# One-hots of the dense tokens' gates: from VectorE and ScalarE to GpSimd

## The chip, the cores and the metric

The kernel runs on one core of a Trainium2 chip. The metric is the device time of one execution in microseconds, lower is better. The time of the kernel before is 4674.65 us, the median of 3 runs (4665.11 to 4679.74).

## What is computed

One inference step of a decoder trunk with one layer: a convolution branch and a gated linear attention branch are merged and added to the input, and then comes a mixer with very many small experts (PEER). 512 prompt tokens and 64 sample tokens, 2048 channels, all float32. The change lies in the mixer:

```python
v1, i1 = lax.top_k(s1, 16)          # s1, s2: scores against 128 keys each, per token and head
v2, i2 = lax.top_k(s2, 16)
cs, ci = lax.top_k(v1 + v2 over all pairs, 16)
e = i1[ci // 16] * 128 + i2[ci % 16]          # 16 experts of 16384 for each of 8 heads
g = jax.nn.softmax(cs)
act = gelu(einsum('tkd,td->tk', u_tab[e], h))
out = einsum('tk,tkd->td', g * act, v_tab[e])
```

So each token uses 128 experts, each with a gate g. A matrix "gate of expert e for token t" has 16384 x tokens entries, 128 of them non-zero per token; expert e is the pair (i1, i2) of two numbers under 128.

## The kernel before

The mixer treats the tokens in two ways, both at the same time.

**Gathered tokens** (256 of the prompt, and 64 more packed as a third tile): for each of a token's 128 experts the row of 2048 numbers is fetched by an indirect DMA, one for 128 tokens at once, into a ring of slots. There are 641 such rows. GpSimd issues the gathers (`gather`, L2044) in order; before each it waits until the row that last lay in the slot has been used. The ring has four slots for the first 264 rows and three after that. VectorE uses the rows: L966 multiplies and sums a u row, L974 adds a weighted v row.

**Dense tokens** (256): all 16384 experts are computed, in 128 blocks of 128 experts. In block b TensorE multiplies the block's part of peer_u with the normed tokens (L738, 16 products of 128x128 by 128x256, each of which shows as two in the records), and GELU follows on ScalarE and VectorE: ScalarE squares (L1911), VectorE L1498, ScalarE Tanh (L1918), VectorE L1512 or L1515, and the result H of the block stays in SBUF. After block 127 the v phase follows (L758), with H as operand. The uT loads come in halves of 512 KB on SyncE's queue (L2253) into the four slots of RA, and so do the peer_v loads (L2255).

**Gates of the dense tokens**: from block G_AT = 63 on, TensorE makes the gate matrix of four tokens behind the u product of each block (L749): for one token the product of two one-hot matrices over its 128 selected experts. One has a 1 at i2 of each, the other the gate at i1; their product has the gate of expert (i1, i2) at its place. The one-hots lie in `ohs`, two buffers (halves) of two tokens, each with two kinds (0: scaled by the gate, 1: plain). They take the fourth slot of RA, so that in this stage uT halves have three. `selT` holds the indices and gates with the selected experts on the partitions, and `iota128` the numbers 0 to 127 in each. Per block and half VectorE compares once for both tokens and kinds (`onehots`, L1478, 128x512), and ScalarE scales kind 0 with the gate by two Copy activations (L1927), and then signals `oh_scaled`. The one-hots of gate step q = b + 1 - G_AT are made in block b, for TensorE in block b + 1; they wait until the gate product of block b has read the buffers before. ScalarE copies the gates out of PSUM (L1915) for the blocks ahead, and VectorE multiplies them into H for the blocks behind (`gate_tokens`, L1488) and, for the block at hand, L1522.

**What sets the order.** The order of each engine is fixed in the program. TensorE: u product of b, gate product, u product of b + 1. Both take the next of four PSUM banks (`banks.take`), which must have been freed: a u product's by `h_ready`, a gate product's by `gm_ready`, both of VectorE. VectorE in block b of this stage: `gate_tokens`, L1498, the one-hots, L1512/L1515, L1522, and then as many rows of the gathered tokens as a credit allows (`paced(work, 4.2)`, a row costs 2.4), one or two. How many rows fall into which block is thus settled when the program is built. GpSimd in this stage has the gathers alone, with a query load, a residual load and a gain load where a tile of gathered tokens ends.

Of the kernel before, what the change touches and what calls it, by code (L numbers as in the profile page):

```python
# [9 lines left out]
ACT = mybir.ActivationFunctionType  # L10
ALU = mybir.AluOpType
AX = mybir.AxisListType

P = 128
# [25 lines left out]
NB = NEXP // P  # L40
# [5 lines left out]
G_AT = NB - ND // 4 - 1  # L46
# [87 lines left out]
def trunk(nc, a, o, seen, final):  # L134
    ctx = ExitStack()
    with ctx:
        def sb(name, shape, dt=F32):
            return ctx.enter_context(nc.sbuf_tensor(name, shape, dt))
# [11 lines left out]
        iota128 = sb("iota128", [P, P])  # L150
# [22 lines left out]
        at = KC  # L173
# [83 lines left out]
        selT = holes[:, 0:12, :].rearrange("p (k h) c -> p k h c", k=3)  # L257
# [7 lines left out]
        ohs = [part_of(RA, 3072 + 512 * i, 2, 2, P) for i in range(2)]  # L265
# [24 lines left out]
        def signal(name):  # L290
# [4 lines left out]
        ps_done, z_ready, scores_ready, kdT_ready, o_ready, os_ready, u_half, v_half, w_half = (  # L295
            signal(s) for s in ("ps_done", "z_ready", "scores_ready", "kdT_ready", "o_ready", "os_ready", "u_half",
                                "v_half", "w_half"))
# [14 lines left out]
        (dve_step, ms1_ready, normT_ready, lg_ready, earg_ready, factors_ready, kdarg_ready, decay_ready, att_ready,  # L312
         rsilu_ready, state_ready, kdm_ready, st_updated, gla_ready, head_zeroed, u_ready, conv_done, centered,
         sd_ready, lned, silu_ready, mergedB_ready, part_ready, merged_ready, resid_ready, ms2_ready, h2_ready,
         routed, shifted, gates_ready, row_used, gelu_arg, ss_g, y_g, arg_u, h_ready, onehot_ready, gm_ready,
         sum_ready, ms3_ready, y_ready, sums_ready) = (
            signal(s) for s in (
                "dve_step", "ms1_ready", "normT_ready", "lg_ready", "earg_ready", "factors_ready", "kdarg_ready",
                "decay_ready", "att_ready", "rsilu_ready", "state_ready", "kdm_ready", "st_updated", "gla_ready",
                "head_zeroed", "u_ready", "conv_done", "centered", "sd_ready", "lned", "silu_ready", "mergedB_ready",  # L320
                "part_ready", "merged_ready", "resid_ready", "ms2_ready", "h2_ready", "routed", "shifted",
                "gates_ready", "row_used", "gelu_arg", "ss_g", "y_g", "arg_u", "h_ready", "onehot_ready", "gm_ready",
                "sum_ready", "ms3_ready", "y_ready", "sums_ready"))

        pool_step, consts_made, iota_made, masks_made, qk_zeroed, qs_zeroed = (
# [18 lines left out]

        banks = Banks(ps, signals, seen, final)
        gelu_due = {}
        weight_order = []
        weight_spent = []

# [12 lines left out]
        own_last = max(m for m in range(2 * G_AT - 2) if slot_of[m] == 3)  # L362
# [428 lines left out]
        def _(dve):  # L791
# [673 lines left out]
                    spare((g, hd, "wq"), (16.0, 12.0)[g])  # L1465


            def onehots(q):
                if q == 0:
                    for t in range(2):  # L1470
                        dve.wait_ge(*selT_ready.at(t))
                    dve.wait_ge(*ps_done.at("u", own_last // 2))
                else:
                    dve.wait_ge(*ps_done.at("g", q - 1))
                for half in range(2):
                    t, n = q // 32, q % 32 * 4 + 2 * half
                    sel = selT[:, 0:2, 2 * t + n // 64, n % 64:n % 64 + 2]
                    onehot_ready.on(dve.tensor_tensor(  # L1478
                        ohs[half], iota128[:, :].unsqueeze(1).unsqueeze(1).to_broadcast([P, 2, 2, P]),
                        sel.unsqueeze(3).to_broadcast([P, 2, 2, P]), ALU.is_equal), q, half)  # L1480


            def gate_tokens(q, n):
                dve.wait_ge(*ps_done.at("g", q))
                dve.wait_ge(*g_copied.at(q))
# [6 lines left out]
            for b in range(NB):  # L1492
                scratch = H[:, b, :] if b <= G_AT else u_work
                bank = banks.of("u", b)
                if b > G_AT:
                    gate_tokens(b - 1 - G_AT, b)
                dve.wait_ge(*sq_u.at(b))
                arg_u.on(dve.scalar_tensor_tensor(out=scratch, in0=scratch, scalar=1.0, in1=bank[:, 0:ND], op0=ALU.add,  # L1498
                                                  op1=ALU.mult), b)
                spare((b, "u"), 0.0)  # L1500
                if b < G_AT - 1:
                    paced(work_1, 3.9)
                    paced(work, 2.8)
                elif b < NB - 2:
                    onehots(b + 1 - G_AT)
                assert b != G_AT - 4 or next(work_1, None) is None
                assert b != G_AT or first_row[1] < row_used.n
                assert b != H_FOURTH - 1 or row_used.n >= FOUR_ROWS
                dve.wait_ge(*tanh_u.at(b))
                done = 4 * max(b - G_AT, 0)  # L1510
                if done:
                    dve_step.on(dve.scalar_tensor_tensor(out=scratch[:, 0:done], in0=scratch[:, 0:done], scalar=1.0,  # L1512
                                                         in1=bank[:, 0:done], op0=ALU.add, op1=ALU.mult))
                if done < ND:
                    ins = dve.scalar_tensor_tensor(out=H[:, b, done:], in0=scratch[:, done:], scalar=1.0,  # L1515
                                                   in1=bank[:, done:ND], op0=ALU.add, op1=ALU.mult)
                if 0 < done < ND:
                    dve_step.on(ins)
                if done:
                    dve.wait_ge(*g_copied.at(b - 1 - G_AT))  # L1520
                    dve.wait_ge(*dve_step.now())
                    ins = dve.tensor_tensor(H[:, b, 0:done], scratch[:, 0:done], H[:, b, 0:done], ALU.mult)  # L1522
                h_ready.on(ins, b)
                banks.free(h_ready, "u", b)
                if G_AT - 1 <= b < NB - 3:
                    paced(work, 4.2)
# [24 lines left out]
        def _(act):  # L1551
            fn = nc.scalar.activation
# [350 lines left out]
            for b in range(NB):  # L1903
                serve((b, "u"))
                scratch = H[:, b, :] if b <= G_AT else u_work
                act.wait_ge(*ps_done.at("u", b))
                if b > G_AT:
                    act.wait_ge(*h_ready.at(b - 1))
                if b == H_FOURTH:
                    act.wait_ge(*row_used.at(FOUR_ROWS - 1))  # L1910
                sq_u.on(fn(scratch, banks.of("u", b)[:, 0:ND], ACT.Square, scale=float(np.sqrt(0.044715))), b)  # L1911
                if b > G_AT:
                    q = b - 1 - G_AT
                    act.wait_ge(*ps_done.at("g", q))
                    g_copied.on(fn(H[:, b:, 4 * q:4 * q + 4],  # L1915
                                   banks.of("g", q).rearrange("p (n i) -> p i n", n=4)[:, b:, :], ACT.Copy), q)
                act.wait_ge(*arg_u.at(b))
                tanh_u.on(fn(scratch, scratch, ACT.Tanh, scale=float(np.sqrt(2.0 / np.pi))), b)  # L1918
                if b == G_AT - 1:
                    sel_keep()  # L1920
                if G_AT - 1 <= b < NB - 2:
                    q = b + 1 - G_AT
                    for half in range(2):
                        act.wait_ge(*onehot_ready.at(q, half))
                        for n in range(2):
                            c = q % 32 * 4 + 2 * half + n
                            ins = fn(ohs[half][:, 0, n, :], ohs[half][:, 0, n, :], ACT.Copy,  # L1927
                                     scale=selT[:, 2, 2 * (q // 32) + c // 64, c % 64:c % 64 + 1])
                        oh_scaled.on(ins, q, half)


            ones_made.on(fn(iota128[:, :], iota128[:, :], ACT.Copy, scale=0.0, bias=1.0))
# [14 lines left out]
        def _(pool):  # L1947
# [45 lines left out]
            def query_load(t):  # L1993
                if t:
                    pool.wait_ge(*y_g.at(before_tile[t]))
                else:
                    pool.wait_ge(*normT_ready.at(1, KT - 1))
                    pool.wait_ge(*x2_stored.at(0))
                n = TOK[t]
                src = (h2_d[0], h2_d[1], h2_d[2, 0:OWN, :])[t]  # L2000
                if t >= 2:
                    pool.wait_ge(*x2_stored.at(1))
                    pool.wait_ge(*h2_stored.at(1))
                for i in range(P // n):
                    key = (t, i) if i < P // n - 1 else (t,)
                    query_in.dma(pool.dma_start(h2cur[i * n:(i + 1) * n, :], src), *key)
                if t:
                    last = before_tile[t]
                    yg_stored.dma(pool.dma_start(y_out[last], cur[0:TOK[last], :]), last)
# [15 lines left out]
            def gather(m):  # L2025
# [13 lines left out]
                if kind == "m":  # L2039
# [5 lines left out]
                    ring[s][:, :], None, (a["peer_u"] if kind == "u" else a["peer_v"])[0],  # L2045
                    bass.IndirectOffsetOnAxis(ap=idx, axis=0), bounds_check=NEXP - 1, oob_is_err=True), m)

            query_load(0)
            for m in range(len(row_list)):
                t = row_list[m][0]  # L2050
                gather(m)
                if m - 3 == last_u[t]:
                    gain_load(t)
                if t and m == first_row[t] + 2:
                    query_load(t)
                if m == first_row[t] + 12:
                    residual_load(t)
# [287 lines left out]
```

## Time and profile before

| | before |
|---|---|
| median of 3 runs | 4674.65 us |
| lowest and highest run | 4665.11, 4679.74 us |
| span of the profiled execution | 4667.9 us |
| TensorE busy | 4588.6 us (98%) |
| VectorE busy | 2713.5 us (58%) |
| ScalarE busy | 539.6 us (12%) |
| GpSimd busy | 956.5 us (20%) |
| DMA moved | 1350.34 MB, 289 GB/s in the mean |

The profile is of one execution, and its own time stands in the table as the span. Busy shares are means over stages that differ much; the stage of the change is the part from 3217 to 3740 us. There are stages before it in which GpSimd and the gathers do nothing, and behind it the v phase, with DMA at its fullest.

### The profile page before, as it was taken

To read this page: it belongs to the slowest core of one execution; us is meant where nothing else is said; L and a number is where in the kernel's file an instruction comes from. 1 tells how busy PE (TensorE), PEld (TensorE's weight loads), DVE (VectorE), ACT (ScalarE), POOL (GpSimd) and SP (SyncE) were. 2 spreads that over 40 slices of the span, in tenths; PEclk is the share of its full clock that TensorE was granted. 3 is DMA by queue.
4 is the path that set the end of the run, shared out by engine and by line. 5 is a ranking of instruction groups with operands and counts; after the bars stand their busy time and mean duration, and the time that the engine had idled before them with its cause. 6 is when DMAs were issued, how large, how long until landed. Compare 5 with 4: busy or idle time off the path is not lost.

```text
span 4667.9 us, 50792 instructions
## 1 busy us (share of the span) xinstructions
PE 4588.6 (98%) x20474; PEld 3719.0 (80%) x20474; DVE 2713.5 (58%) x4679; ACT 539.6 (12%) x1229; POOL 956.5 (20%) x691
## 2 busy tenths in 40 slices
PE   8999999999999999999999999999999999999998
PEld 7888888888767676667776678888888888888887
DVE  4434500017678686745556658886788855556552
ACT  1111200000111111010000111112222200000000
POOL 1000000000112313014443332222332323222220
PEclk9999999999999999999999999999999999999999
DMA  4434444545669779659999888888999999999994
GB/s 174 139 133 140 172 147 155 176 172 178 219 237 334 290 266 350 221 211 361 362 370 377 332 327 327 329 332 323 346 356 345 348 380 410 395 413 420 421 417 164
DMA packets 264157, 1350.34 MB, mean 289 GB/s; under 512 B 45729, under 2 KB 52129, under 8 KB 140338
## 3 DMA queue, kind: packets, MB, share of 16 engines
q1 hardware_dynamic: 170066, 663.90, 38.9%
q0 software_dynamic: 93856, 683.19, 37.0%
q8 instruction: 162, 2.65, 0.2%
q14 instruction: 73, 0.60, 0.0%
HBM read 1306.30 MB, written 40.16 MB: 288 GB/s over the span
## 4 chain that ended last, share of the span: by engine, by line
PE 87%; DMA 8%; DVE 3%; issue 1%; ACT 0%; POOL 0%; DVEq 0%; POOLq 0%; ACTq 0%
PE ps L404 39%; PE ps L738 16%; PE ps L758 9%; PE pm L758 9%; PE ps L563 4%; DMA RA<-in_uT 4%; PE ps L625 2%; DMA RA<-in_peer_v 2%; DMA RING<-in_peer_u,table 2%; PE ps L518 1%; PE pm L511 1%; PE pm L467 1%; PE ps L571 1%; DVE BIG L1252 1%; DMA BIG<-in_peer_v,table 1%
## 5 line engine op out<-in xcount | busy, mean ns | idle before, releaser
L404 PE MATMUL ps<-X,BIG 128*128 128x320 f32 (+1 forms) x5632 | 1394.9, 409 | 7.5 <-DVE X L1444 4.2
L404 PEld LDWEIGHTS ps<-X,BIG 128*128 128x128 f32 x5632 | 1068.4, 190 | 317.6 <-issue 10.0
L738 PE MATMUL ps<-X,RA 128*128 128x256 f32 x4096 | 902.2, 380 | 20.9 <-DMA RA<-in_uT 20.7
L738 PEld LDWEIGHTS ps<-X,RA 128*128 128x128 f32 x4096 | 772.6, 190 | 131.6 <-DMA RA<-in_uT 22.6
L974 DVE SCALAR_TENSOR_TENSOR CUR<-RING,wexp,CUR 128x2048 f32<-128x2048 f32 x288 | 676.8, 2350 | 258.0 <-DMA RING<-in_peer_v,table 150.3
L966 DVE CUSTOM_DVE_ANT_0 RING<-RING,CUR 128x2048 f32<-128x2048 f32 x286 | 652.0, 2289 | 280.0 <-DMA RING<-in_peer_u,table 146.9
L2044 POOL DMA_INDIRECT RING<-in_peer_u,table x222 | 352.3, 1587 | 951.1 <-DVE hidden L966 644.0
L2044 POOL DMA_INDIRECT RING<-in_peer_v,table x224 | 332.1, 1483 | 920.1 <-DVE CUR L974 746.5
L404 PE MATMUL ps<-BIG 128*128 128x256 f32 (+1 forms) x2048 | 504.4, 408 | 7.9 <-DVE BIG L1430 5.6
L404 PEld LDWEIGHTS ps<-BIG 128*128 128x128 f32 x2048 | 389.9, 191 | 117.8 <-DVE BIG L1430 7.0
L758 PE MATMUL ps<-BIG,RA 128*128 128x256 f32 x2048 | 465.4, 380 | 8.7 <-DMA RA<-in_peer_v 8.7
L758 PE MATMUL pm<-BIG,RA 128*128 128x256 f32 x2048 | 463.4, 379 | 1.5 <-DVE BIG L1488 1.3
L758 PEld LDWEIGHTS ps<-BIG,RA 128*128 128x128 f32 x2048 | 389.6, 191 | 64.9 <-DMA RA<-in_peer_v 11.9
L758 PEld LDWEIGHTS pm<-BIG,RA 128*128 128x128 f32 x2048 | 388.6, 190 | 56.2 <-DMA RA<-in_peer_v 1.8
L1345 DVE SCALAR_TENSOR_TENSOR BIG<-BIG,ps 128x256 f32<-128x256 f32 (+1 forms) x32 | 14.6, 455 | 426.0 <-PE ps L404 426.0
L1252 DVE SCALAR_TENSOR_TENSOR BIG<-BIG 128x256 f32<-128x256 f32 x720 | 240.4, 412 | 0.1
L563 PE MATMUL ps<-BIG,X 128*128 128x256 f32 x1024 | 223.4, 379 | 0.0
L563 PEld LDWEIGHTS ps<-BIG,X 128*128 128x128 f32 x1024 | 194.2, 190 | 28.2 <-issue 1.5
L1984 POOL MEMSET BIG<- 128x1024 f32 x1 | 1.0, 952 | 914.5 <-DVE BIG L1362 914.5
L404 PE MATMUL ps<-RA,BIG 128*128 128x256 f32 (+1 forms) x512 | 128.6, 410 | 3.9 <-issue 3.9
L404 PEld LDWEIGHTS ps<-RA,BIG 128*128 128x128 f32 x512 | 98.1, 192 | 32.1 <-issue 5.9
L625 PE MATMUL ps<-BIG 128*128 128x256 f32 x512 | 110.8, 379 | 1.3 <-DVE BIG L1362 1.3
(317 smaller groups left out, 3082.5 us busy)
## 6 DMA issues: line engine op xcount, KB each, us to landing
BIG<-in_w_in_b SPq DMA_DIRECT2D x128, 1024.0 KB, 5.8
RA<-in_uT SPq DMA_DIRECT2D x256, 512.0 KB
RA<-in_peer_v SPq DMA_DIRECT2D x256, 512.0 KB
BIG<-in_w_gb_b SPq DMA_DIRECT2D x32, 1024.0 KB, 5.1
BIG<-in_w_ga_b SPq DMA_DIRECT2D x32, 1024.0 KB, 4.9
BIG<-in_w_gla_o_b SPq DMA_DIRECT2D x32, 1024.0 KB, 5.0
BIG<-in_w_mix_b SPq DMA_DIRECT2D x32, 1024.0 KB, 6.7
BIG<-in_w_q_b SPq DMA_DIRECT2D x32, 1024.0 KB, 8.1
```

What stands on the lines that cost most here:

```text
L404: last = pe.matmul(bank[:, 0:n], w(k, j * P, P), src[:, k, 0:n], start=(k == 0), stop=(k == kt - 1))
L467: last = pe.matmul(lev_ps[0:n, l, 0:n], kk, qq, start=(j == 0), stop=(j == 1))
L511: last = pe.matmul(pm[0:NS, 2, :], qs[:, j, b * NS:(b + 1) * NS], sring[:, b % 4, j, :], start=False, stop=(b == DEC_B - 1 and j == 1))
L518: last = pe.matmul(bank, kdm[0:NS, b % 2, j * P:(j + 1) * P], vt[0:NS, 2, :], start=True, stop=True)
L563: last = pe.matmul(bank[:, c * PAIR:(c + 1) * PAIR], normT[g][:, k, span(c)], w(k, 0, PAIR), start=(k == 0), stop=(k == KT - 1))
L625: last = pe.matmul(bank[:, c * PAIR:(c + 1) * PAIR], merged[0][:, k, span(c)], w(k, 0, PAIR), start=(k == 0), stop=(k == KT - 1))
L738: last = pe.matmul(bank[:, 0:ND], half_slot[slot_of[m]][:, k % 8, :], h2T[1][:, k, 0:ND], start=(k == 0), stop=(k == KT - 1))
L758: last = pe.matmul(v_sums[half][:, i, :], vhalf[slot_of[m]][:, i * P:(i + 1) * P], H[:, b, :], start=(b == 0 and i % 2 == 0), stop=(b == N ...
L966: row_used.on(dve.tensor_tensor_reduce(out=row, in0=row, in1=h2cur[0:n, :], scale=1.0, scalar=0.0, op0=ALU.mult, op1=ALU.add, accum_out=hi ...
L974: row_used.on(dve.scalar_tensor_tensor(out=cur[0:n, :], in0=row, scalar=wexp[0:n, par, k:k + 1], in1=cur[0:n, :], op0=ALU.mult, op1=ALU.ad ...
L1252: ins = dve.scalar_tensor_tensor(out=out, in0=src, scalar=w, in1=out, op0=ALU.mult, op1=ALU.add)
L2044: row_loaded[s].dma(pool.indirect_dma_start(ring[s][:, :], None, (a["peer_u"] if kind == "u" else a["peer_v"])[0], bass.IndirectOffsetOnAx ...
```

## The change

The comparisons leave VectorE and the scalings leave ScalarE. GpSimd makes each 128x128 one-hot by one tensor_scalar: iota128 is compared with the index on each partition, and for kind 0 a second operation of the same instruction multiplies with the gate. That is 8 instructions per block instead of 2 on VectorE and 4 on ScalarE. They wait for the same things as before (the gate product that read the buffers last) and signal `oh_scaled` themselves. When VectorE's program is built, it notes at each place where the one-hots were how many rows it has used (`rows_before_onehot`). GpSimd's program puts the one-hots in front of the first gather whose number is over that: with m rows used, the gather of row m still goes ahead of them, and the gather of row m + 1 comes behind.

```diff
-            def onehots(q):
-                ...
-                    dve.wait_ge(*ps_done.at("g", q - 1))
-                for half in range(2):
-                    t, n = q // 32, q % 32 * 4 + 2 * half
-                    sel = selT[:, 0:2, 2 * t + n // 64, n % 64:n % 64 + 2]
-                    onehot_ready.on(dve.tensor_tensor(
-                        ohs[half], iota128[:, :].unsqueeze(1).unsqueeze(1).to_broadcast([P, 2, 2, P]),
-                        sel.unsqueeze(3).to_broadcast([P, 2, 2, P]), ALU.is_equal), q, half)
...
                 elif b < NB - 2:
-                    onehots(b + 1 - G_AT)
+                    rows_before_onehot.append(row_used.n)
...
-                if G_AT - 1 <= b < NB - 2:
-                    q = b + 1 - G_AT
-                    for half in range(2):
-                        act.wait_ge(*onehot_ready.at(q, half))
-                        for n in range(2):
-                            c = q % 32 * 4 + 2 * half + n
-                            ins = fn(ohs[half][:, 0, n, :], ohs[half][:, 0, n, :], ACT.Copy,
-                                     scale=selT[:, 2, 2 * (q // 32) + c // 64, c % 64:c % 64 + 1])
-                        oh_scaled.on(ins, q, half)
...
+            def onehots(q):
+                if q == 0:
+                    for t in range(2):
+                        pool.wait_ge(*selT_ready.at(t))
+                    pool.wait_ge(*ps_done.at("u", own_last // 2))
+                else:
+                    pool.wait_ge(*ps_done.at("g", q - 1))
+                for half in range(2):
+                    for n in range(2):
+                        c = q % 32 * 4 + 2 * half + n
+                        at = 2 * (q // 32) + c // 64, c % 64
+                        for kind in range(2):
+                            gate = selT[:, 2, at[0], at[1]:at[1] + 1] if kind == 0 else None
+                            ins = pool.tensor_scalar(
+                                ohs[half][:, kind, n, :], iota128[:, :], selT[:, kind, at[0], at[1]:at[1] + 1], gate,
+                                ALU.is_equal, *((ALU.mult,) if kind == 0 else ()))
+                    oh_scaled.on(ins, q, half)
...
             for m in range(len(row_list)):
                 t = row_list[m][0]
+                while q < len(rows_before_onehot) and m > rows_before_onehot[q]:
+                    onehots(q)
+                    q += 1
                 gather(m)
```

## Rows read from the trace of the kernel before

**Rows 1.** The page: busy time (share of the span) and instructions of each engine.

```profile
PE 4588.6 (98%) x20474; PEld 3719.0 (80%) x20474; DVE 2713.5 (58%) x4679; ACT 539.6 (12%) x1229; POOL 956.5 (20%) x691
```

**Rows 2.** The page: the chain of work that ended last, by engine.

```profile
PE 87%; DMA 8%; DVE 3%; issue 1%; ACT 0%; POOL 0%; DVEq 0%; POOLq 0%; ACTq 0%
```

**Rows 3.** Gate products: ns min/median/max, first and last start; in 3217:3737 busy, mean | idle.

```profile
L749 PE MATMUL ps<-RA x512: 272/275/275, 3220.9 to 3740.3; 128*128 128x128 f32 x171
...
L749 PE MATMUL ps<-RA 128*128 128x128 f32 x504 | 66.4, 275 | 0.0
```

**Rows 4.** The chain in order of time, 3395 to 3440: start us, us, what.

```profile
3399.21 3.72 PE ps L738 x16
3402.93 0.89 PE ps L749 x8
3403.82 6.91 PE ps L738 x32
...
3430.71 8.38 DMA RA<-in_uT
```

**Rows 5.** Waits in 3217:3737: engine line <- releaser: us in total, times, longest us.

```profile
DVE RING L966 <- DMA RING<-in_peer_u,table: 23.0, 14, 2.9
...
PE ps L738 <- DMA RA<-in_uT: 19.1, 19, 2.2
...
DVE CUR L974 <- DMA RING<-in_peer_v,table: 9.3, 6, 3.0
```

**Rows 6.** Timeline of one block: start us, us, engine, line, what [idle before <- releaser].

```profile
3406.35 2.28 DVE L966 CUSTOM_DVE_ANT_0 RING<-RING,CUR 128x2048 f32<-128x2048 f32 x1
...
3408.57 2.29 DVE L966 CUSTOM_DVE_ANT_0 RING<-RING,CUR 128x2048 f32<-128x2048 f32 x1
3409.44 2.29 POOL L2044 DMA_INDIRECT RING<-in_peer_u,table  x1 [5.21 <-DVE hidden L966]
...
3411.44 0.52 DVE L1488 TENSOR_TENSOR BIG<-ps,BIG 128x344 f32<-128x344 f32 x1 [0.58 <-issue]
...
3411.87 0.41 DVE L1498 SCALAR_TENSOR_TENSOR table<-table,ps 128x256 f32<-128x256 f32 x1
3412.04 1.01 POOL L2044 DMA_INDIRECT RING<-in_peer_u,table  x1 [0.30 <-issue]
3412.20 1.29 DVE L1478 TENSOR_TENSOR RA<-iota,X 128x512 f32<-128x512 f32 x2
3412.32 0.42 ACT L1918 ACTIVATE table<-table 128x256 f32<-128x256 f32 x1 [0.97 <-DVE table L1498]
...
3413.40 0.24 DVE L1512 SCALAR_TENSOR_TENSOR table<-table,ps 128x92 f32<-128x92 f32 x1
...
3414.16 2.29 DVE L966 CUSTOM_DVE_ANT_0 RING<-RING,CUR 128x2048 f32<-128x2048 f32 x1
...
3417.60 2.29 DVE L966 CUSTOM_DVE_ANT_0 RING<-RING,CUR 128x2048 f32<-128x2048 f32 x1 [1.15 <-DMA RING<-in_peer_u,table]
```

**Rows 7.** The stage: us, busy us (instructions) of each engine, TensorE clock, DMA share, GB/s.

```profile
3217.00:3737.00 520.00, 500.75 (x2528) 440.81 (x2528) 422.89 (x623) 144.76 (x447) 158.13 (x109) 1.00 0.92 347
```

**Rows 8.** Groups in 3217:3737: shapes, count | busy us, mean ns | idle before, releaser.

```profile
L966 DVE CUSTOM_DVE_ANT_0 RING<-RING,CUR 128x2048 f32<-128x2048 f32 x58 | 132.0, 2288 | 23.1 <-DMA RING<-in_peer_u,table 23.0
L974 DVE SCALAR_TENSOR_TENSOR CUR<-RING,wexp,CUR 128x2048 f32<-128x2048 f32 x51 | 119.8, 2349 | 11.0 <-DMA RING<-in_peer_v,table 9.3
...
L1927 ACT ACTIVATE RA<-RA,X 128x128 f32<-128x128 f32 x256 | 82.9, 394 | 13.0 <-DVE RA L1478 13.0
L1478 DVE TENSOR_TENSOR RA<-iota,X 128x512 f32<-128x512 f32 x128 | 82.7, 687 | 1.4 <-ACT X L1873 1.3
```

**Rows 9.** GpSimd's arithmetic of the size: ns min/median/max, first and last start.

```profile
L1977 POOL COPY BIG<-ident x1: 292/292/292, 14.3 to 14.3; 128x128 f32<-128x128 f32 x1
...
L1975 POOL TENSOR_SCALAR_AFFINE_SELECT BIG<-BIG x12: 294/370/714, 8.3 to 13.5; 128x128 f32<-128x128 f32 x12
```

**Rows 10.** Timeline of VectorE near the end: the last row of the gathered tokens.

```profile
4560.71 2.35 DVE L974 SCALAR_TENSOR_TENSOR CUR<-RING,wexp,CUR 128x2048 f32<-128x2048 f32 x1 [1.35 <-DMA RING<-in_peer_v,X]
```

More of the change, by code:

```diff
@@ L314, in trunk @@
          sd_ready, lned, silu_ready, mergedB_ready, part_ready, merged_ready, resid_ready, ms2_ready, h2_ready,
-         routed, shifted, gates_ready, row_used, gelu_arg, ss_g, y_g, arg_u, h_ready, onehot_ready, gm_ready,
+         routed, shifted, gates_ready, row_used, gelu_arg, ss_g, y_g, arg_u, h_ready, gm_ready,
          sum_ready, ms3_ready, y_ready, sums_ready) = (
@@ L321, in trunk @@
                 "part_ready", "merged_ready", "resid_ready", "ms2_ready", "h2_ready", "routed", "shifted",
-                "gates_ready", "row_used", "gelu_arg", "ss_g", "y_g", "arg_u", "h_ready", "onehot_ready", "gm_ready",
+                "gates_ready", "row_used", "gelu_arg", "ss_g", "y_g", "arg_u", "h_ready", "gm_ready",
                 "sum_ready", "ms3_ready", "y_ready", "sums_ready"))
@@ L346, in trunk @@
         gelu_due = {}
+        rows_before_onehot = []
         weight_order = []
@@ L1465, in _ @@
                     spare((g, hd, "wq"), (16.0, 12.0)[g])
-            def onehots(q):
[L1469 to L1473, printed above, removed]
-                    dve.wait_ge(*ps_done.at("g", q - 1))
-                for half in range(2):
-                    t, n = q // 32, q % 32 * 4 + 2 * half
-                    sel = selT[:, 0:2, 2 * t + n // 64, n % 64:n % 64 + 2]
-                    onehot_ready.on(dve.tensor_tensor(
-                        ohs[half], iota128[:, :].unsqueeze(1).unsqueeze(1).to_broadcast([P, 2, 2, P]),
-                        sel.unsqueeze(3).to_broadcast([P, 2, 2, P]), ALU.is_equal), q, half)
             def gate_tokens(q, n):
@@ L2046, in gather @@
                     bass.IndirectOffsetOnAxis(ap=idx, axis=0), bounds_check=NEXP - 1, oob_is_err=True), m)
+            def onehots(q):
[15 more added lines that the diff above has]
+                    oh_scaled.on(ins, q, half)
             query_load(0)
+            q = 0
             for m in range(len(row_list)):
                 t = row_list[m][0]
+                while q < len(rows_before_onehot) and m > rows_before_onehot[q]:
+                    onehots(q)
+                    q += 1
                 gather(m)
```

## Prediction

> **What bounds the kernel now.** I read the page first. TensorE is busy in 98% of the span [rows 1] and holds 87% of the chain that ended last [rows 2], so only what delays TensorE costs time. The change touches one stage, the 64 expert blocks 63 to 126, in which each block has an up-projection product (L738) and then a gate product (L749) that reads the one-hots. The first of its 512 gate matmuls starts at 3220.9 us and the last at 3740.3 [rows 3], so 63 periods take 519.4 - 0.9 = 518.5 us, 8.23 us each. The chain shows an undisturbed period: 0.89 us of L749 and 6.91 of L738, 7.80 us [rows 4]. The other 0.43 us per block, 27 us in all, are TensorE's waits for the uT loads, 19.1 us of idle [rows 5], and the restarts behind them (the half product behind a load takes 3.72 us, against half of 6.91 [rows 4]). TensorE never waited for a one-hot or for a bank: neither stands among the waits of the stage, and L749 has no idle time in front of it [rows 3, 5]. So **the comparisons and the scaling are hidden today**, and removing them cannot by itself give anything.
>
> Then I looked at what the three engines do in a block [rows 6]. VectorE is busy 423 of 520 us [rows 7], and its largest work is one or two expert rows per block (L966, L974; 58 and 51 rows in the stage, 1.7 per block, 2.3 us each [rows 8]). GpSimd does only gathers, 109 of them [rows 7], and spends most of its time waiting for a ring slot. Each row needs its gather, and there are three slots.
>
> **What is removed.** VectorE loses 128 comparisons of 0.687 us, two per block, which take 1.29 us together; ScalarE loses 256 scalings of 0.394 us [rows 6, 8]. Where they overlap they are busy for 82.7 and 82.9 us of the stage [rows 8]. In the block of [rows 6] the first comparison starts when L1498 ends; without the two, L1512 would wait for the Tanh only, which ends at 3412.74, and start at 3412.8, not 3413.4. The u product ended at 3410.73 [rows 4], so VectorE's first row starts 2.9 us after it and not 3.4. All this lies beside TensorE: gain 0.
>
> **What is added.** GpSimd gets 8 tensor_scalar of 128x128 per block. The trace has none. Nearest rows on GpSimd: the copy of 128x128 takes 0.292 us, and an affine select of that size 0.294 to 0.714 in 12 cases, 0.370 in the median [rows 9]. A comparison against a per-partition value is nearest to the select, and half of the new instructions do a second operation; I take **0.40 us**, a little over the median select, and keep 0.29 and 0.71 as ends. Eight are 3.2 us (2.3 to 5.7).
>
> They don't run undisturbed. A gather takes 1.00 us when VectorE does no row, but 2.29 us when it comes up in the middle of one: that of 3409.44 ends at 3411.73, 0.9 us after the row that ran to 3410.86; the next, at 3412.04, takes 1.01 [rows 6]. So a GpSimd instruction that reads SBUF is held until a row operation, with its two inputs in SBUF, is through. I take the same for the new ones, since they read iota128 and selT: a row in their midst adds up to 2.3 us. The Trainium skill has this as a rule (SBUF — State Buffer, Who interferes with whom: a VectorE instruction with two SBUF inputs contends with a GpSimd instruction that reads SBUF); for the gathers this trace agrees, for arithmetic no row shows it. By the rule 8 one-hots need 3.2 to 5.5 us, without it 3.2.
>
> **The new wait, and what is queued behind it.** GpSimd now waits in each block for the gate product, because the one-hot buffers are single. On its in-order queue the gathers stand behind. With m the first row that VectorE uses in block b, the order is gather m, one-hots, gather m+1 (and m+2). Today gather m+1 goes out 0.8 us after its slot is free; a gather that was released at 3408.65 is used at 3417.60, and that row still waited for its data, 1.15 us [rows 6]. In the change gather m+1 goes out only after one-hots, some 5 to 7 us later, and VectorE's second row of the block, then its whole next block (banks of u and g), wait for it. Who waits for that: a u product takes the bank of the u product two blocks back, freed by VectorE. The query, residual and gain loads on that queue keep their places against rows already used, and cost nothing. SyncE's queue isn't touched.
>
> I walk seven blocks with 2, 2, 1, 2, 2, 1 rows, as the stage has them. Terms: u 6.91, g 0.89; VectorE's work before its rows ends 2.9 after the u product, or takes 2.25 when VectorE is late (0.52 + 0.41, 0.6 for the Tanh, 0.76 from L1512 to the row, less gaps); row 2.3; gather 1.0, 0.3 to the next, landing 5.9 after its end (3411.73 to 3417.60); 0.8 from a freed slot to the gather [rows 6]. Zero is the end of a u product. Block 0: g to 0.89, one-hots from 1.15, held by the row of 3.15 to 5.45, done at 6.65; gather of the second row ends 7.65 and lands 13.55; that row ends 15.85 (today about 8). Block 1: VectorE frees its bank at 18.0, while TensorE wants it at 16.5; the g product of block 2 has to wait until 16.35, for a bank, the next u product until 18.0. One-hots of block 2 lie between rows and end at 25.55, 0.65 after TensorE wants them. Carried on, the u products end at 0, 7.8, 15.6, 24.9, 33.4, 41.2, 49.3: in the mean **8.22**, that is 0.42 of new wait per block over 7.80. Most of it is for banks, some for one-hots, and behind a single-row block VectorE catches up.
>
> Of today's 0.43 us for the uT loads some goes under these waits, since a standing TensorE lets loads land. DMA is 92% busy in the stage [rows 7], so not all of it goes: I let two thirds stay, 0.29. Sum: 7.80 + 0.42 + 0.29 = 8.51, against 8.23: 0.28 x 63 = **+17.6 us**. Behind the stage nothing changes: the plan hands the same rows to the same blocks, and the last row ends at 4563, 105 us before the span does [rows 10]. The profiled execution of before spans 4667.9 us, 6.75 under the median 4674.65 of its runs; I add that: 4674.65 + 17.6 = 4692.
>
> **The rivals.**
> Heavy: GpSimd becomes the bound. It decides from about 0.5 us per instruction. Then its own work per block is 8 x 0.5 = 4.0, 1.7 gathers x 1.45 (158 us over 109 [rows 7]) = 2.5, and 2.3 held by a row: 8.8 us, +0.57 x 63 = +36 us; at 0.71 it is 5.7 + 2.5 + 2.3 = 10.5, +143 us. I set it at +60: 4735. For it: half of the new instructions have two operations, and both take two pointers' worth of operands. Against it: 0.292 for the copy. 22%.
> Hidden: 0.3 us per instruction or no hold by rows. Then one-hots are ready 2.4 to 3.2 us after g, gather m+1 lands by 11.5, the row ends 13.8, the bank is free at 16.0, before 16.5. New waits vanish, and the time is 4675, within 5. 26%.
> Faster: the same small price, and the gathers, held back by one-hots, leave uT loads a freer path. Its place is the three-slot ring of uT halves, whose loads stand on the chain for 8.38 us [rows 4] where two halves and at most one g product give 6.9 to 7.8. It decides if a load gets 0.6 us shorter; it gives at most the 27 us, and I price it at two thirds, -18: 4657. Against it: the bytes per block stay, and two gathers in a bunch load DMA more at once. 14%.
> My forecast of +17.6 has 38%, its own range +5 to +35.
>
> **How the numbers follow.** 0.3%, about what a measurement of this kernel can tell from no change, is 14 us. Slower: the heavy case and four fifths of the forecast's, 0.22 + 0.30 = 0.52. Same: the hidden case and the rest, 0.34. Faster: 0.14. For 8 in 10 the range goes down to 4660, into the faster case, and up to 4750, which leaves out the upper third of the heavy one.
>
> **What would show it.** L749 with idle in front of it, released by GpSimd, means late one-hots; L738 with idle from a VectorE release means banks, so late gathers. DMA idle in front of L966 and L974, 32 us in the stage [rows 5], should grow to over 150. The new POOL group should show 512 instructions at 0.40 us, longer ones beside rows. The first to last start of L749 should be 536 us. If the mean is under 0.3, or TensorE's clock (1.00 in the mean now, the higher of its two levels [rows 7]) falls in the new waits, I am wrong in size; if the DMA waits of L738 vanish without new ones, in sign.

## The result, and the profile after

The changed kernel takes 4830.18 us (median of 4 runs, 4823.18 to 4832.06), the kernel before in the same comparison 4677.01 us (median of 4). The ratio is 1.0335, with a 95% interval of 1.0322 to 1.0349: **153 us slower**, where 17.6 were forecast and the range ended at 4750.

The page of the kernel after: the busy row, and the chain that ended last by engine and by line (rows 1 and 2 of before). Lines have moved: L739 is L738 of before, L750 is L749, L967 and L975 are L966 and L974, L2021 is L2044, and L2038 is the new tensor_scalar.

```profile
PE 4654.4 (96%) x20474; PEld 3756.8 (78%) x20474; DVE 2646.4 (55%) x4551; ACT 456.3 (9%) x973; POOL 1442.0 (30%) x1203
...
PE 78%; POOL 11%; DMA 5%; DVE 3%; issue 3%; ACT 0%; DVEq 0%; POOLq 0%; ACTq 0%
PE ps L405 37%; PE ps L739 9%; POOL RA L2038 9%; PE ps L759 9%; PE pm L759 8%; PE ps L564 4%; PE ps L626 2%; DMA RING<-in_peer_u,table 2%; POOL RING L2021 2%; DMA RA<-in_peer_v 2%; PE ps L519 1%; PE pm L512 1%; PE pm L468 1%; PE ps L572 1%; DVE BIG L1253 1%
```

GpSimd wasn't on the chain before [rows 2] and now holds 11% of it, and TensorE's share of the chain went from 87 to 78%.

The gate products of after (ns min/median/max, first and last start), and the groups of the stage, 3217 to 3900 us (count | busy us, mean ns of one | idle before them and its releasers):

```profile
L750 PE MATMUL ps<-RA x512: 272/275/582, 3221.9 to 3898.8; 128*128 128x128 f32 x171
...
L2038 POOL TENSOR_SCALAR RA<-iota,X 128x128 f32<-128x128 f32 x512 | 507.7, 1001 | 16.3 <-ACT X L1859 11.8 <-PE ps L750 1.6
...
L967 DVE CUSTOM_DVE_ANT_0 RING<-RING,CUR 128x2048 f32<-128x2048 f32 x58 | 135.0, 2327 | 148.7 <-DMA RING<-in_peer_u,table 148.5 <-issue 0.2
L975 DVE SCALAR_TENSOR_TENSOR CUR<-RING,wexp,CUR 128x2048 f32<-128x2048 f32 x51 | 122.2, 2395 | 134.0 <-DMA RING<-in_peer_v,table 133.9
L750 PE MATMUL ps<-RA 128*128 128x128 f32 x512 | 91.6, 313 | 111.1 <-POOL RA L2038 56.5 <-DVE BIG L1474 54.1
```

The stage accounts for nearly all of the loss. First to last start is 676.9 us, less 0.9 and over 63: a **period of 10.73 us**, where before it was 8.23 [rows 3]; 2.5 x 63 = 157.5 us of the 162.4 by which the profiled span is longer. The last gate matmul begins 158.5 us later than in before. The tensor_scalars take 1.00 us in the mean, and L750, which never waited [rows 3], now has 111 us of idle in front of it, half released by GpSimd (late one-hots) and half by VectorE (a gate bank not free).

The stage as a whole (length, busy us and instructions of PE, PEld, DVE, ACT and POOL, clock, DMA share, GB/s), its first half:

```profile
3217.00:3560.00 343.00, 286.23 (x1287) 242.75 (x1287) 173.34 (x249) 32.50 (x97) 326.75 (x315) 0.93 0.75 266
```

GpSimd is busy 95% of it; in before it was 158 us of 520 [rows 7]. VectorE fell from 81 to 51%, DMA from 92 to 75%. So **GpSimd is the bound of the stage**. TensorE's granted clock went from 1.00 to 0.93 of its higher level; a u product behind a wait took 8.80 us where others take 7.07. That can have cost next to nothing: from 3217 to 3900 us GpSimd's one-hots waited for a gate product 1.6 us in all, and its gathers for VectorE 2.1.

GpSimd in two blocks of after, the rows of VectorE that lie in them and a u product (timeline: start us, us, engine):

```profile
3439.61 5.48 POOL L2038 TENSOR_SCALAR RA<-iota,X 128x128 f32<-128x128 f32 x8
3444.83 2.29 DVE L967 CUSTOM_DVE_ANT_0 RING<-RING,CUR 128x2048 f32<-128x2048 f32 x1 [6.17 <-DMA RING<-in_peer_u,table]
...
3448.37 1.03 POOL L2021 DMA_INDIRECT RING<-in_peer_u,table  x1 [0.30 <-issue]
...
3449.13 2.37 DVE L967 CUSTOM_DVE_ANT_0 RING<-RING,CUR 128x2048 f32<-128x2048 f32 x1
...
3449.27 8.80 PE L739 MATMUL ps<-X,RA 128*128 128x256 f32 x32 [0.51 <-DVE BIG L1508]
...
3449.44 11.00 POOL L2038 TENSOR_SCALAR RA<-iota,X 128x128 f32<-128x128 f32 x8
...
3452.36 2.31 DVE L967 CUSTOM_DVE_ANT_0 RING<-RING,CUR 128x2048 f32<-128x2048 f32 x1 [0.84 <-DMA RING<-in_peer_u,table]
...
3456.70 2.50 DVE L967 CUSTOM_DVE_ANT_0 RING<-RING,CUR 128x2048 f32<-128x2048 f32 x1
```

The eight of 3439.61 meet no row but for their last 0.26 us, and take 5.48 us. The eight of 3449.44 meet three rows and take 11.00. That made two things to test: what an instruction costs, and what a row beside it adds.

### The profile page after: what moved, and what is told of

It reads as the page before. It is cut to its first block, busy times and chain, and to the rows that moved or that the text cites. A ratio compares the mean times of both kernels' runs of the same rounds, so it can differ in the third digit from the quotient of the medians.

```text
span 4830.3 us, 50920 instructions
## 1 busy us (share of the span) xinstructions
PE 4654.4 (96%) x20474; PEld 3756.8 (78%) x20474; DVE 2646.4 (55%) x4551; ACT 456.3 (9%) x973; POOL 1442.0 (30%) x1203
## 4 chain that ended last, share of the span: by engine, by line
PE 78%; POOL 11%; DMA 5%; DVE 3%; issue 3%; ACT 0%; DVEq 0%; POOLq 0%; ACTq 0%
PE ps L405 37%; PE ps L739 9%; POOL RA L2038 9%; PE ps L759 9%; PE pm L759 8%; PE ps L564 4%; PE ps L626 2%; DMA RING<-in_peer_u,table 2%; POOL RING L2021 2%; DMA RA<-in_peer_v 2%; PE ps L519 1%; PE pm L512 1%; PE pm L468 1%; PE ps L572 1%; DVE BIG L1253 1%
## 5 line engine op out<-in xcount | busy, mean ns | idle before, releaser
L739 PE MATMUL ps<-X,RA 128*128 128x256 f32 x4096 | 935.5, 391 | 3.5 <-DVE BIG L1508 3.4
L739 PEld LDWEIGHTS ps<-X,RA 128*128 128x128 f32 x4096 | 800.9, 197 | 120.3 <-DVE BIG L1508 5.8
L975 DVE SCALAR_TENSOR_TENSOR CUR<-RING,wexp,CUR 128x2048 f32<-128x2048 f32 x288 | 679.1, 2358 | 383.3 <-DMA RING<-in_peer_v,table 272.2
L967 DVE CUSTOM_DVE_ANT_0 RING<-RING,CUR 128x2048 f32<-128x2048 f32 x286 | 654.8, 2297 | 399.3 <-DMA RING<-in_peer_u,table 262.6
L2021 POOL DMA_INDIRECT RING<-in_peer_u,table x222 | 343.5, 1547 | 748.8 <-DVE hidden L967 481.8
L2021 POOL DMA_INDIRECT RING<-in_peer_v,table x224 | 318.0, 1420 | 771.9 <-DVE CUR L975 614.3
L2038 POOL TENSOR_SCALAR RA<-iota,X 128x128 f32<-128x128 f32 x512 | 507.7, 1001 | 16.3 <-ACT X L1859 11.8
L750 PE MATMUL ps<-RA 128*128 128x128 f32 x512 | 91.6, 313 | 111.1 <-POOL RA L2038 56.5
L750 PEld LDWEIGHTS ps<-RA 128*128 128x128 f32 x512 | 75.7, 209 | 132.9 <-POOL RA L2038 65.4
```

The lines of the kernel that those rows point to most:

```text
L739: last = pe.matmul(bank[:, 0:ND], half_slot[slot_of[m]][:, k % 8, :], h2T[1][:, k, 0:ND], start=(k == 0), stop=(k == KT - 1))
L750: last = pe.matmul(bank[:, n * P:(n + 1) * P], ohs[n // 2][:, 1, n % 2, :], ohs[n // 2][:, 0, n % 2, :], start=True, stop=True)
L967: row_used.on(dve.tensor_tensor_reduce(out=row, in0=row, in1=h2cur[0:n, :], scale=1.0, scalar=0.0, op0=ALU.mult, op1=ALU.add, accum_out=hi ...
L975: row_used.on(dve.scalar_tensor_tensor(out=cur[0:n, :], in0=row, scalar=wexp[0:n, par, k:k + 1], in1=cur[0:n, :], op0=ALU.mult, op1=ALU.ad ...
L2021: row_loaded[s].dma(pool.indirect_dma_start(ring[s][:, :], None, (a["peer_u"] if kind == "u" else a["peer_v"])[0], bass.IndirectOffsetOnAx ...
L2038: ins = pool.tensor_scalar(ohs[half][:, kind, n, :], iota128[:, :], selT[:, kind, at[0], at[1]:at[1] + 1], gate, ALU.is_equal, *((ALU.mult ...
```

## Theories

**H**, GpSimd's time: eight tensor_scalars have 5.5 us of their own, rows with two SBUF inputs hold them for 2.5 more, gathers take 2.3 and gaps 0.4, together 10.7. **L**, the order: gathers stand behind the one-hots and come too late; VectorE waits for its rows and TensorE for its banks, and the price of an instruction matters only through this. In both, the waits of after would look much the same.

## The experiments

Ratios are against the kernel before on the same chip, with 95% intervals. The period is worked out as above, from the first and last start of the gate products.

**One-input rows.** On the changed kernel; the two one-hots also stand on lines of their own here and below, L2032 with two operations and L2034 with one.

```diff
-row_used.on(dve.tensor_tensor_reduce(out=row, in0=row, in1=h2cur[0:n, :], ...
+row_used.on(dve.tensor_reduce(hidden[0:n, par, k:k + 1], row, AX.X, ALU.add), m)
-row_used.on(dve.scalar_tensor_tensor(out=cur[0:n, :], in0=row, scalar=wexp..., in1=cur[0:n, :], ...
+row_used.on(dve.tensor_reduce(wexp[0:n, par, k:k + 1], row, AX.X, ALU.add), m)
```

> Built on the changed kernel. Every row operation of the gathered tokens (L966/L974 of before, two inputs in SBUF) is replaced by a sum over the row, one input in SBUF, of about the same length (2.1 to 2.3 us); so the hidden values and the sums of the gathered tokens are left out, their gathers and waits stay. Theory H (GpSimd is the bound of the stage, and a third of its time it is held by row operations with two SBUF inputs): the tensor_scalars fall from 1.00 us in the mean to 0.69, the price that eight in a row show when no row is near (5.48 us); GpSimd then has 5.5 + 1.7 gathers of 1.0 + 0.6 of gaps = 7.8 us per block, so the period falls from 10.7 to 8.0 to 8.4 us and the time to between 4665 and 4700 us. Theory L (the late gathers set the period, the hold is a side effect of any busy VectorE): the tensor_scalars stay near 1.0 us, the period over 9.8, the time over 4770.

Measured: 4689.93 us, ratio 1.0051 (1.0032 to 1.0069); period 8.59 us. The two lines of the tensor_scalars (ns min/median/max):

```profile
L2032 POOL TENSOR_SCALAR RA<-iota,X x256: 786/796/1025, 3214.0 to 3756.7; 128x128 f32<-128x128 f32 x128
...
L2034 POOL TENSOR_SCALAR RA<-iota,X x256: 589/591/651, 3214.8 to 3757.4; 128x128 f32<-128x128 f32 x128
```

H holds for the size of the hold: with the second SBUF input of the rows gone, 142 of the 162 us of span are gone, though VectorE still does a row operation in the same places. The period is over the 8.0 to 8.4 that I expected: VectorE still waits 143 us of 500 for rows, and the experiment with these rows and the gathers first, below, shows that this is the order. The run also gives the undisturbed price: **0.80 us with two operations, 0.59 with one**, 4 x 1.39 = 5.5 us per block. Of 8 x 1.00 us in after, 2.5 are thus hold.

**Gathers first.**

```diff
-while q < len(rows_before_onehot) and m > rows_before_onehot[q]:
+while q < len(rows_before_onehot) and m > rows_before_onehot[q] + 2:
```

> The changed kernel, but with up to two more gathers ahead of the one-hots of a block on GpSimd's queue, so that VectorE's rows of this block and the first of the next don't wait for one-hots. Theory H (GpSimd's own time is the bound, 8 one-hots x 1.0 + 1.7 gathers x 1.3): the sum is the same, so the period stays at 10.2 to 10.9 us and the time at 4800 to 4845; VectorE's waits for rows shrink and TensorE's waits for one-hots grow instead. Theory L (late gathers): the period falls under 9.3 and the time under 4745.

Measured: 4841.44 us, ratio 1.0366 (1.0337 to 1.0394); period 10.95 us, a little over the range, from two runs. As H says: the order alone gives nothing back while GpSimd's time is the bound. Its first waits of 3230 to 3730 us (engine line <- releaser: us in total, times, longest), and a stretch of the timeline of GpSimd and of VectorE:

```profile
PEld ps L750 <- POOL RA L2038: 101.5, 40, 5.5
PE ps L750 <- POOL RA L2038: 100.0, 50, 5.3
DVE RING L967 <- DMA RING<-in_peer_u,table: 67.2, 16, 6.4
```

```profile
3462.02 4.66 POOL L2036 TENSOR_SCALAR RA<-iota,X 128x128 f32<-128x128 f32 x1
3466.67 0.59 POOL L2038 TENSOR_SCALAR RA<-iota,X 128x128 f32<-128x128 f32 x1
...
3461.59 2.28 DVE L967 CUSTOM_DVE_ANT_0 RING<-RING,CUR 128x2048 f32<-128x2048 f32 x1
...
3463.80 2.28 DVE L967 CUSTOM_DVE_ANT_0 RING<-RING,CUR 128x2048 f32<-128x2048 f32 x1
```

VectorE's waits for rows fall (67 + 30 us in this window, 215 in after) and TensorE's waits for one-hots grow, 40 to 100 us. GpSimd is busy 475 of the 500 us, as in after (477). The timeline shows the hold in its clearest form: one tensor_scalar of 0.8 us takes 4.66, since two rows follow each other without a gap; it ends 0.6 us after the second. GpSimd doesn't get in between.

**Kind split.** GpSimd makes the scaled one-hots alone; VectorE compares the plain ones.

```diff
+onehot_ready.on(dve.tensor_tensor(ohs[half][:, 1, :, :], iota128 ... , sel ... , ALU.is_equal), q, half)
...
-for kind in range(2):
-    ...
-    ins = pool.tensor_scalar(ohs[half][:, kind, n, :], iota128[:, :], selT[:, kind, ...], gate, ALU.is_equal, ...)
+ins = pool.tensor_scalar(ohs[half][:, 0, n, :], iota128[:, :], selT[:, 0, ...], selT[:, 2, ...], ALU.is_equal, ALU.mult)
```

> The whole computation. GpSimd makes only the scaled one-hots (kind 0, four instructions with two operations per block, gate multiplied in), VectorE compares the plain ones (kind 1, one instruction for two tokens, 128x256), ScalarE does nothing for them. Theory H: GpSimd has 4 x 0.77 = 3.1 us of its own, up to 2.5 of hold and 1.7 x 1.3 of gathers, 7.8 us, just under TensorE's period with its load waits (8.23): 4670 to 4700 us. Theory L: the gathers still stand behind the one-hots, which end at most 2 us earlier, so that a third at least of the 153 us stays: over 4725.

Measured: 4762.19 us, ratio 1.0203 (1.0182 to 1.0224); period 9.53 us. H's 4670 to 4700 is missed, and L's "over 4725" met. GpSimd is busy 396 of 500 us and no longer the bound, and yet 95 us are lost. The four instructions take 1.23 us each: half as many, but 0.44 us of hold in each instead of 0.31, so the hold doesn't go with their number. The waits of 3230 to 3730 us:

```profile
DVE CUR L976 <- DMA RING<-in_peer_v,table: 89.0, 23, 8.4
DVE RING L968 <- DMA RING<-in_peer_u,table: 82.4, 24, 8.0
PEld ps L751 <- DVE BIG L1489: 60.0, 21, 5.6
PE ps L751 <- DVE RA L1480: 52.7, 23, 5.2
```

VectorE waits 171 us for rows, and TensorE for VectorE: for a gate bank (L1489), and for the plain one-hots (L1480) that VectorE makes again, as in before. This is L, which H had hidden.

**Kind split, gathers first.** Both edits.

> The split of the kinds again (GpSimd the scaled one-hots, VectorE the plain ones), with up to two more gathers ahead of GpSimd's one-hots. With the split alone the period was 9.53 us and GpSimd 79% busy, VectorE waiting 171 us of 500 for rows. Theory H alone (GpSimd's own time) doesn't explain that; theory L (gathers behind the one-hots come too late for VectorE, whose banks TensorE waits for) says that with the gathers ahead VectorE's waits for rows fall under 60 us, and the period to 8.2 to 8.6 us: 4665 to 4695 us. If instead the hold of GpSimd by VectorE's rows makes one-hots late, the period stays over 9.2 and TensorE's waits for GpSimd grow: over 4730.

Measured: 4725.88 us, ratio 1.0121 (1.0090 to 1.0152); period 9.09 us. Between the two expectations: VectorE's waits for rows fell to 55 us, as L said, and 36 us came back. What is left I put down to hold. From 3230 to 3730 us:

```profile
L2052 POOL TENSOR_SCALAR RA<-iota,X 128x128 f32<-128x128 f32 x221 | 340.2, 1545 | 10.2 <-PE ps L751 8.1
```

The mean tensor_scalar is now 1.55 us, GpSimd busy 451 of 500 us, and TensorE waits for it (33 us). With data at hand VectorE does its rows right behind each other; the longest tensor_scalar takes 5.19 us, so one was held for up to 4.4.

**One-input rows, gathers first.** Hold and order both taken away.

> One-input rows and the gathers ahead of the one-hots, both at once (gathered tokens' sums left out). With one-input rows alone the period was 8.59 us and VectorE waited 143 us of 500 for rows. If the two causes are GpSimd's held time and the late gathers, and no third, nothing is left: period 8.1 to 8.3 us, waits for rows under 60 us, 4660 to 4680 us. If TensorE waits for one-hots instead, since 5.5 us and two gathers come before they are ready, the period stays at 8.5 and more: over 4685.

Measured: 4676.15 us, ratio 1.0017 (1.0007 to 1.0028); period 8.25 us, against 8.23 of before [rows 3]; all as expected.

```profile
L750 PE MATMUL ps<-RA x512: 272/275/377, 3217.5 to 3738.2; 128*128 128x128 f32 x171
```

VectorE's waits for rows are 45 us of 500. So with eight tensor_scalars of 5.5 us on GpSimd the stage is as short as before once the hold and the order are gone: the two causes together are enough, and 5.5 us of own time are not by themselves too much.

**Write only.** Does a row hold every instruction of GpSimd, or those that read SBUF?

```diff
-ins = pool.tensor_scalar(ohs[half][:, kind, n, :], iota128[:, :], selT..., gate, ALU.is_equal, ...)
+for i in range(3):
+    step(pool.memset(ohs[half], 0.0))
+ins = pool.memset(ohs[half], 0.0)
```

> The changed kernel with each half's four tensor_scalars (read and write SBUF) replaced by four memsets of 128x512, each waiting for the one before (write only; so the gates and all dense experts are left out). Alone a memset of this size takes 0.52 us (0.95 for 1024 columns and 0.21 for 128, in the profile), eight of them with their waits 4.9 us per block, against 5.5 of the tensor_scalars. If VectorE's rows hold only what reads SBUF through the shared interface, the memsets stay within 10% of 0.52 us, GpSimd needs 4.9 + 2.2 of gathers, and the period is 8.3 to 8.8 us, 4675 to 4715 us, as with one-input rows. If they hold every GpSimd instruction, the memsets take 0.8 us and more in the mean and the period is over 9.5, over 4750 us.

Measured: 4718.09 us, ratio 1.0096 (1.0058 to 1.0134); period 9.04 us. The memsets (ns min/median/max), and three of them in the midst of a row:

```profile
L2034 POOL MEMSET RA<- x384: 525/525/550, 3223.0 to 3794.1; 128x512 f32 x192
L2035 POOL MEMSET RA<- x128: 525/525/528, 3224.8 to 3794.7; 128x512 f32 x128
```

```profile
3442.04 2.28 DVE L967 CUSTOM_DVE_ANT_0 RING<-RING,CUR 128x2048 f32<-128x2048 f32 x1
3442.23 1.71 POOL L2034 MEMSET RA<- 128x512 f32 x3
```

None of 512 is held, the longest takes 0.55 us. The hold is one of reads: the copies below do no arithmetic but read SBUF, and they are held. The Trainium skill says so (SBUF — State Buffer, Who interferes with whom: a VectorE instruction with two SBUF inputs contends with a GpSimd instruction that reads SBUF, not with one that only writes it). These runs agree at both ends: 1.00 us against 0.70 in the mean for tensor_scalars with two-input and one-input rows, 0.525 throughout for memsets. The time and the period are over what I expected (4675 to 4715 us, 8.3 to 8.8); I put that down to L, 158 us of waits for rows in 500. Why the period is 9.04 here and 8.59 with one-input rows stays open; the gathers, which are held here (1.31 us against 1.05), are part of it.

**Copies.** The price alone brought to the low end of my bounds.

```diff
-ins = pool.tensor_scalar(ohs[half][:, kind, n, :], iota128[:, :], selT..., gate, ALU.is_equal, ...)
+ins = pool.tensor_copy(ohs[half][:, kind, n, :], iota128[:, :])
```

> The changed kernel with each tensor_scalar replaced by a copy of 128x128 from iota128 into the same place (reads and writes SBUF as before; the comparison and the gates are left out). Alone such a copy takes 0.29 us, so this is the change at the low end of the price that I had bounded, with the two-input rows and the order of the gathers as in the change. GpSimd's own time falls from 5.5 to 2.3 us per block; with up to 2.3 of hold and 2.2 to 2.5 of gathers it isn't the bound. If the price was what decided, the period falls from 10.73 to between 8.3 and 9.1 us, what remains being the late gathers: 4675 to 4725 us. If the hold grows to fill the time (more than one row per block holds GpSimd), the period stays over 9.5 and the time over 4750.

Measured: 4685.99 us, ratio 1.0036 (1.0024 to 1.0048), 16.7 us over before; period 8.29 us.

```profile
L2037 POOL COPY RA<-iota x512: 279/288/2451, 3221.0 to 3746.3; 128x128 f32<-128x128 f32 x171
```

The hold is still there, 0.47 us in the mean where 0.29 is the price, and so is the order, but GpSimd has time for both (it is busy 347 of the 500 us from 3230): the period is within 0.1 us of before. So the price decides, through GpSimd's sum. Of the 16.7 us the stage's profile explains 8 at most. The profiled execution was the fastest of the eight, 11 us under their median, and where the others lost the rest isn't known.

**Immediates.** What of the price comes from the operands; with one-input rows. The form with one operation gets the constant 5.0 too.

```diff
-tensor_scalar(..., iota128[:, :], selT[:, 0, ...], selT[:, 2, ...], ALU.is_equal, ALU.mult)
+tensor_scalar(..., iota128[:, :], 5.0, 0.25, ALU.is_equal, ALU.mult)
```

> The kernel with one-input rows again, with the operands of the tensor_scalars as constants instead of per-partition values from selT (so the gates are left out as well). It measures what a per-partition operand costs. With them it was 0.796 us for two operations and 0.590 for one. If each costs about 0.1 us to read, the two become 0.6 and 0.5; if the loop over 128 columns is what costs (copy of 128x128: 0.29 us), they stay within 0.05 us of 0.796 and 0.590.

Measured: 0.647 us with two operations and 0.532 with one, in 4706.75 us (one run); period 8.76. So of 0.796 us two per-partition operands are 0.15, and one of 0.59 is 0.06, between my two cases. The rest is 0.29 for a copy, 0.24 more for a comparison, 0.12 for a second operation. With 15% less of its own time on GpSimd the period isn't shorter than 8.59, as fits a GpSimd that isn't the bound with one-input rows; why it is longer stays open.

**Three tries to be faster than before**, on the kernel before, by the 27 us that TensorE loses to the uT loads. The first gives fewer rows to the stage (`paced`) and more to the v phase (`V_PACE`):

```diff
-paced(work, 4.2)
+paced(work, 3.6)
-V_PACE = 3.65
+V_PACE = 3.8
```

> The kernel before with the credit of rows per block in the stage cut from 4.2 to 3.6 us and V_PACE raised from 3.65 to 3.8: some 15 rows move from the stage to the v phase. It asks what the 27 us are that TensorE loses there to uT loads. If they come from the gathers' share of the DMA (92% busy), a seventh less gathering takes away a third or more of them, and the v phase, whose rows end 105 us before the span, hides the moved rows: 4655 to 4668 us. If they come from the three-slot ring alone, 4675.

Measured: 4658.90 us, ratio 0.9977 (0.9967 to 0.9986); period 8.04 us. Of 3230 to 3730 us, TensorE's waits for loads, in before 16.9 us, are now

```profile
PE ps L738 <- DMA RA<-in_uT: 8.1, 10, 1.9
```

Faster by 9 to 11 us: a small gain clear of noise. In the stage the DMA share fell from 0.92 to 0.86. The v phase up to 4560 us was full already (0.98 to 1.01) and stays so; the rows that left the stage found room behind that, where the share rose from 0.43 to 0.69.

The second goes on, to 3.0 in the stage and from 2.8 to 3.1 before it.

> The kernel before with the rows spread further: 3.1 us of credit per block before the stage instead of 2.8, 3.0 in it instead of 4.2, V_PACE 3.8. Cutting 4.2 to 3.6 took the period of the stage from 8.23 to 8.04 us and TensorE's waits for uT loads from 19 to 8 us. If it goes on in proportion the waits fall under 3 us and the period to 7.9: 4645 to 4657 us. If the v phase is hurt by the moved rows (its DMA is 100% busy), nothing is gained over 4659.

Measured: 4685.83 us, ratio 1.0033 (1.0019 to 1.0047). The period fell on, to 7.93 us, but the time rose: 7 rows more than with 3.6 lie behind the stage, and from 4400 us on the chain that ended last is now that of the gathered rows:

```profile
by line: DMA RING<-in_peer_v,X 44.0%; DMA RING<-in_peer_u,X 18.6%; DVE CUR L974 13.6%; issue 7.4%; DVE RING L966 4.9%; PE pm L772 3.2%; DVE X L1546 2.2%; DMA RING<-CUR 1.5%; PE ps L758 1.2%; DVE CUR L970 0.8%; DVE RING L989 0.8%; DVE BIG L1
```

The third has 3.1 before the stage, 3.6 in it and `V_PACE` as it was.

> The kernel before with 3.1 us of credit before the stage and 3.6 in it, V_PACE left at 3.65. 3.6 in the stage gave 0.23% with V_PACE 3.8; 3.0 lost it again, with TensorE's waits in the last part of the v phase, where rows had been moved to. If the v phase is what limits, taking the rows into the blocks before the stage (DMA 86% busy) keeps the gain or adds to it: 4650 to 4660. If the first u blocks are no better a place, 4665 and more.

Measured: 4661.28 us, ratio 0.9988 (0.9975 to 1.0000); period 8.02. Between the two expectations, and no better than 3.6 and 3.8. The 105 us between the last row and the end [rows 10] are what can be spent, and 3.6 with 3.8 leaves 46 of them.

## Why the prediction was wrong

**Right.** Comparisons and scaling were hidden and their removal gave nothing. The hold of a GpSimd read by a two-input row was read from one gather of 2.29 us [rows 6], carried over to arithmetic that no row showed, and holds there. The queue argument was right too: gathers behind the one-hots, VectorE late, TensorE waiting for banks, though for those of the gate products (L750) and hardly for those of the u products (L739, 3.4 us). DMA idle in front of the row operations was to grow from 32 to over 150 us; it is 282 in the stage. The rest of the kernel is as it was. The period that the forecast started from, and its sum, come out as written, but for the 536 us, which should be 537.

**Where it failed: the price.** "I take 0.40 us, a little over the median select." It is 0.69 in the mean, 0.59 and 0.80. I read the affine select as nearest by the kind of work and took its median of 0.37; but half of the new instructions do one operation more, and all read per-partition operands, which the select doesn't. That isn't all of it: with constants one operation still takes 0.53. The upper end of 0.71 that I kept from the slowest select would have been the better value. With it eight cost 5.5 us and not 3.2, and GpSimd's sum goes over TensorE's period. The shape of the loss is another, too: not 0.42 us per block of waits for late gathers and one-hots, but 2.5 us by which GpSimd's work and its gaps exceed TensorE's period.

The forecast was a walk of waits in which GpSimd always had time left. It never set GpSimd's sum against the period at its own 0.40: by the rival's formula that is 3.2 + 2.5 + 2.3 = 8.0 of 8.23 us, with nothing for gaps. The rival I called heavy had the true mechanism, the sum of GpSimd's own time. I let it decide "from about 0.5 us per instruction", and its own formula at 0.69 is 5.5 + 2.5 + 2.3 = 10.3 us, +131 us. Measured are 5.5 of price, 2.5 of hold (I had 2.3), 2.3 of gathers and 0.4 of gaps that I had left out: 10.7. But I priced the case at +60, below what its formula gave over most of its span, and closed the range at 4750, in the midst of it: by the formula that leaves out nearly two thirds of the span of 0.5 to 0.71, not a third. That was the second fault. A range over the whole case, to +143 (4818), would still have ended 12 us short of 4830; the gaps, 0.4 x 63 = 25 us, are what the formula lacked.

TensorE's clock, which I named as a sign of being wrong in size, did fall, to 0.93 in the stage. But GpSimd waited for TensorE hardly at all, so the clock isn't where the 135 us beyond the forecast come from.

**The terms apart.** From the medians: hold by two-input rows, about 140 us (after against one-input rows, 4830 and 4690); the order, 14 to 16 us more (one-input rows 1.0051, with gathers first 1.0017; 21 by the two profiled spans); and what is left is 0.2%. They don't simply add: each of the two shows its size only when the other no longer covers it. At a price of 0.29 us the whole change costs 17 us, as the copies show, which is by chance the figure I forecast for 0.40. No run has a price of 0.40, so whether the walk would have come out there isn't shown.

## To carry to other kernels

When work moves to an engine that looks idle (20% busy here, 30% in the stage), sum that engine's time for one period of the stage, with what it already has there and with what holds it, and set it against the period; do this over the whole range of an unknown price, and let the range of the time follow. The idle share of an engine that issues gathers isn't free either: whatever is put on its in-order queue delays them. An operation that reads SBUF on GpSimd costs its price plus the rest of any two-input VectorE operation that it meets, and the whole of the next if that follows without a gap, so it fits beside one-input work and badly beside long two-input rows.

## What the runs showed of the hardware

- A GpSimd tensor_scalar of 128x128 float32 takes 0.59 us with one operation and 0.80 with two, with per-partition operands; 0.53 and 0.65 with constants. A copy takes 0.29. A gather that GpSimd issues takes 1.05 us in the mean beside one-input rows and 1.31 beside two-input rows and memsets.
- Two VectorE operations of 2.3 us with two SBUF inputs, one right behind the other, hold a GpSimd read through both: 4.66 us for one of 0.8; the longest of any run takes 5.19. That GpSimd isn't let in between I hadn't expected.
- Memsets on GpSimd beside the same rows keep to 0.525 us, 512 of them.
- It goes the other way as well, but less: the row operations grew from 2.288 to 2.327 and from 2.349 to 2.395 us in the mean [rows 8], with single ones of 2.5. Beside the memsets, which don't read, they stayed at 2.290 and 2.348.
